# Stick-breaking softplus tiles split into a high and a low half for the triangle sums, with buffers laid out per phase

## The reference

```python
def block(i):                       # 128 queries
    z = jnp.einsum('bqhd,bshd->bhqs', qb, k).astype(jnp.float32) * dh ** -0.5
    ok = ((kpos[None, :] < qpos[:, None]) & valid[None, :])[None, None]
    log_1m = jnp.where(ok, -jax.nn.softplus(z), 0.0)
    after = lax.cumsum(log_1m, axis=3, reverse=True) - log_1m
    w = jnp.where(ok, jnp.exp(jax.nn.log_sigmoid(z) + after), 0.0)
    return jnp.einsum('bhqs,bshd->bqhd', w.astype(v.dtype), v)
od = stick_breaking(hd(dq, 8), hd(dk, 8), hd(dv, 8), valid)
od = od.reshape(bsz, P, -1) * jax.nn.silu(dg)
return jnp.concatenate([oc, od], axis=-1) @ w_out
```

## Time and profile before

| | |
|---|---|
| timed runs, median of 3 | 2760.39 us (2758.14 to 2762.59) |
| profiled execution | 2754.39 us, span 2752.6 us |
| TensorE matmul busy | 2623.4 us, 95% of the span |
| DVE / ACT / GpSimd busy | 38% / 32% / 39% |
| mean granted TensorE clock | 0.986 of full speed |
| the eight phases of stick-breaking | about 645 to 811 us |

### The profile page before, as it was taken

The page is one execution under the profiler, slowest core; times in us unless marked ns, Lnnn a source line. Parts: engine busy times, 40 slices in busy tenths (PEclk is TensorE's granted clock), DMA queues, the critical chain, the costliest instruction groups (busy, mean ns, idle before and its releaser), DMA issues.

```text
span 2752.6 us, 32062 instructions
## 1 busy us (share of the span) xinstructions
PE 2623.4 (95%) x13245; PEld 2134.7 (78%) x13245; DVE 1033.9 (38%) x1742; ACT 881.1 (32%) x1289; POOL 1068.3 (39%) x830
## 2 busy tenths in 40 slices
PE   7999898999996999999789999999999999999999
PEld 6888787886655888877667888878888888888887
DVE  4655355224335312145554222243121444421212
ACT  4432333225543222232534222232222322322221
POOL 3232232331114444443204444444444444454443
PEclk9999999999998999999999999999999999999999
DMA  4122001220012233221102332233322232223322
GB/s 129 59 62 82 28 24 54 77 77 32 23 39 91 89 94 105 92 87 59 58 9 92 100 97 94 88 96 98 101 92 92 92 104 95 92 92 95 104 92 77
DMA packets 215851, 217.78 MB, mean 79 GB/s; under 512 B 10599, under 2 KB 213090, under 8 KB 215706
## 3 DMA queue, kind: packets, MB, share of 16 engines
q1 hardware_dynamic: 215504, 215.68, 24.5%
q10 hardware_dynamic: 202, 0.06, 0.0%
HBM read 213.60 MB, written 2.12 MB: 78 GB/s over the span
## 4 chain that ended last, share of the span: by engine, by line
PE 86%; DVE 5%; ACT 4%; issue 2%; POOL 2%; DMA 1%; ACTq 0%; DVEq 0%; SPq 0%
PE ps L490 65%; PE ps L486 7%; PE ps L493 3%; POOL wl L466 2%; PE ps L804 2%; PE ps L773 1%; ACT wh L459 1%; PE ps L2021 1%; PE ps L1999 1%; PE ps L788 1%; DVE score L1587 1%; PE ps L2415 1%; DVE top L1586 0%; PE ps L1483 0%; PE ps L1980 0%
## 5 line engine op out<-in xcount | busy, mean ns | idle before, releaser
L466 POOL TENSOR_TENSOR wl<-raw,wh 128x512 fp32r<-128x512 f32 x794 | 1039.6, 1340 | 1591.3 <-ACT wh L459 1591.3
L490 PE MATMUL ps<-NH,wh 128*128 128x512 f32 (+1 forms) x1824 | 720.8, 395 | 38.1 <-POOL wl L466 27.8
L490 PE MATMUL ps<-NL,wh 128*128 128x512 f32 (+1 forms) x1824 | 715.4, 392 | 0.0
L490 PE MATMUL ps<-NH,wl 128*128 128x512 f32 (+1 forms) x1824 | 714.8, 392 | 0.0
L459 ACT ACTIVATE wh<-raw 128x2048 fp32r<-128x2048 f32 (+4 forms) x219 | 380.3, 1737 | 459.9 <-PE ps L490 413.6
L490 PEld LDWEIGHTS ps<-NH,wh 128*128 128x128 f32 (+1 forms) x1824 | 344.9, 189 | 119.9 <-POOL wl L466 30.9
L490 PEld LDWEIGHTS ps<-NH,wl 128*128 128x128 f32 (+1 forms) x1824 | 344.7, 189 | 74.3
L490 PEld LDWEIGHTS ps<-NL,wh 128*128 128x128 f32 (+1 forms) x1824 | 344.9, 189 | 73.6 <-issue 1.4
L490 PE MATMUL ps<-GH,wh 128*128 128x512 f32 x832 | 330.0, 397 | 3.0 <-DVE GL L728 2.3
L490 PE MATMUL ps<-GH,wl 128*128 128x512 f32 x832 | 332.6, 400 | 0.0
L490 PE MATMUL ps<-GL,wh 128*128 128x512 f32 x832 | 329.1, 396 | 0.0
(11 more groups left out here) (389 smaller groups left out, 3074.7 us busy)
## 6 DMA issues: line engine op xcount, KB each, us to landing
raw<-in_ffn_w_gate SPq DMA_DIRECT2D x44, 1024.0 KB, 5.3
raw<-in_ffn_w_up SPq DMA_DIRECT2D x44, 1024.0 KB, 5.3
raw<-in_ffn_w_down SPq DMA_DIRECT2D x32, 1024.0 KB, 4.9
raw<-in_w_in_ab SPq DMA_DIRECT2D x16, 1024.0 KB, 5.6
raw<-in_w_in_cd SPq DMA_DIRECT2D x14, 1024.0 KB, 5.0
raw<-in_ffn_w_down SPq DMA_DIRECT2D x16, 768.0 KB, 4.2
raw<-in_c_w_in SPq DMA_DIRECT2D x12, 1024.0 KB, 5.0
raw<-in_w_out_ab SPq DMA_DIRECT2D x8, 512.0 KB, 3.5
```

Of the source, the lines that this page charges most:

```text
L466: ins = nc.gpsimd.tensor_tensor(wl[:, b % 2, ks, 0:w], raw[:, b % 2, ks, 0:w], wh[:, b % 2, ks, 0:w].bitcast(F32), ALU.subtract)
L490: last = nc.tensor.matmul(ps[0:m1 - m0, bank, 0:SEQ], w[:, s, k, m0:m1], x(k), start=start, stop=stop)
```

## The change

The four softplus tiles of a phase are split. ACT copies each into `soft_hi` in F32R, DVE subtracts it from the tile in place into `soft_lo`, which lies over `soft`. The triangle product of line 1999 and the 128-column product of line 2001 are each done twice, on the high and on the low half, with copies of the constants in F32R. TensorE waits for `sb_soft_low`, no longer for `sb_soft`. The products on `later` stay as they are. Odd and even phases now use the same columns of `soft`, and `later` is laid out in 1152 columns instead of 1408.

```diff
-    soft = at("soft", 33984, [P, 2, 1920])
-    later = at("later", 37824, [P, 2, 1408])
+    soft = at("soft", 33984, [P, 2, 1152])
+    soft_lo = at("soft_lo", 33984, [P, 2, 1152], F32R)
+    soft_hi = at("soft_hi", 36288, [P, 2, 1024], F32R)
+    suffix_r = at("suffix_r", 51584, [P, P], F32R)
+    minus_r = at("minus_r", 51712, [P, P], F32R)
+    later = at("later", 38336, [P, 2, 1152])
...
-    SOFT_AT = ((128, 512), (512, 896), (896, 1408), (1408, 1920))
+    SOFT_AT = ((128, 512), (512, 896), (128, 640), (640, 1152))
...
-                pe.wait_ge(S("sb_soft"), n + 1)
-                nc.tensor.matmul(o[:, 0:w], const("suffix", 0, kn, kn), soft[0:kn, h, a:b], start=False, stop=False, skip_group_check=True)
+                pe.wait_ge(S("sb_soft_low"), n + 1)
+                nc.tensor.matmul(o[:, 0:w], suffix_r[0:kn, 0:kn], soft_hi[0:kn, h, a - P:b - P], start=False, stop=False, skip_group_check=True)
+                nc.tensor.matmul(o[:, 0:w], suffix_r[0:kn, 0:kn], soft_lo[0:kn, h, a:b], start=False, stop=False, skip_group_check=True)
                 if part == 0:
-                    last = nc.tensor.matmul(o[:, 256:384], const("minus_one"), soft[:, h, 128:256], start=False, stop=True, skip_group_check=True)
+                    nc.tensor.matmul(o[:, 256:384], minus_r[:, :], soft_hi[:, h, 0:P], start=False, stop=False, skip_group_check=True)
+                    last = nc.tensor.matmul(o[:, 256:384], minus_r[:, :], soft_lo[:, h, P:2 * P], start=False, stop=True, skip_group_check=True)
...
+        def low(n):
+            p, h, part = sb_task(n)
+            a, b = SOFT_AT[part]
+            kn = sb_rows(part)
+            dve.wait_ge(S("sb_soft_high"), n + 1)
+            if part < 3:
+                dve.wait_ge(S("sb_later"), 6 * p + 2 * part + h + 1)
+            nc.vector.tensor_tensor(soft_lo[0:kn, h, a:b], soft[0:kn, h, a:b], soft_hi[0:kn, h, a - P:b - P].bitcast(F32), ALU.subtract).then_inc(S("sb_soft_low"), 1)
...
-                    ins = nc.vector.memset(later[:, h, 384:512], 0.0)
+                    ins = nc.vector.memset(later[:, h, 512:640], 0.0)
+                nc.vector.tensor_copy(suffix_r[:, :], const("suffix"))
+                ins = nc.vector.tensor_copy(minus_r[:, :], const("minus_one"))
                 step(dve, ins)
             for g in range(2):
                 softplus(4 * f + 2 * g)
...
                     carry(f, 2 * (f % 2) + g, 1)
+            for j in range(4):
+                low(4 * f + j)
             for b, i in sb_between(f):
...
             if f == 0:
                 lin_high(act, ret, NT)
+            for j in range(4):
+                n = 4 * f + j
...
+                act.wait_ge(S("sb_soft"), n + 1)
+                nc.scalar.activation(soft_hi[0:kn, h, a - P:b - P], soft[0:kn, h, a:b], ACT.Copy).then_inc(S("sb_soft_high"), 1)
             for b, i in sb_between(f):
                 cd_act(act, b, i)
```

More of the change, by code:

```diff
@@ L1997, in sums @@
                 o = ps[0:kn, j, :]
-                pe.wait_ge(S("sb_soft"), n + 1)
-                nc.tensor.matmul(o[:, 0:w], const("suffix", 0, kn, kn), soft[0:kn, h, a:b], start=False, stop=False, skip_group_check=True)
+                pe.wait_ge(S("sb_soft_low"), n + 1)
+                nc.tensor.matmul(o[:, 0:w], suffix_r[0:kn, 0:kn], soft_hi[0:kn, h, a - P:b - P], start=False, stop=False, skip_group_check=True)
+                nc.tensor.matmul(o[:, 0:w], suffix_r[0:kn, 0:kn], soft_lo[0:kn, h, a:b], start=False, stop=False, skip_group_check=True)
                 if part == 0:
-                    last = nc.tensor.matmul(o[:, 256:384], const("minus_one"), soft[:, h, 128:256], start=False, stop=True, skip_group_check=True)
+                    nc.tensor.matmul(o[:, 256:384], minus_r[:, :], soft_hi[:, h, 0:P], start=False, stop=False, skip_group_check=True)
+                    last = nc.tensor.matmul(o[:, 256:384], minus_r[:, :], soft_lo[:, h, P:2 * P], start=False, stop=True, skip_group_check=True)
                 elif part == 1:
                     pe.wait_ge(S("sb_later"), 6 * p + h + 1)
-                    last = nc.tensor.matmul(o[:, 128:384], const("minus_one"), later[:, h, 128:384], start=False, stop=True, skip_group_check=True)
+                    last = nc.tensor.matmul(o[:, 128:384], const("minus_one"), later[:, h, 640:896], start=False, stop=True, skip_group_check=True)
                 elif part == 2:
                     pe.wait_ge(S("sb_later"), 6 * p + 2 + h + 1)
-                    last = nc.tensor.matmul(o[:, 128:512], const("minus_one"), later[:, h, 512:896], start=False, stop=True, skip_group_check=True)
+                    last = nc.tensor.matmul(o[:, 128:512], const("minus_one"), later[:, h, 128:512], start=False, stop=True, skip_group_check=True)
                 else:
                     pe.wait_ge(S("sb_later"), 6 * p + 4 + h + 1)
-                    last = nc.tensor.matmul(o, const("minus_one", 0, kn), later[:, h, 896:1408], start=False, stop=True, skip_group_check=True)
+                    last = nc.tensor.matmul(o, const("minus_one", 0, kn), later[:, h, 640:1152], start=False, stop=True, skip_group_check=True)
                 last.then_inc(S("sb_sum"), 1)
@@ L2062, in carry @@
             if part == 0:
-                ins = nc.vector.tensor_tensor(later[:, h, 128:384], soft[:, h, 256:512], soft[:, h, 0:256], ALU.add)
+                ins = nc.vector.tensor_tensor(later[:, h, 640:896], soft[:, h, 256:512], soft[:, h, 0:256], ALU.add)
             elif part == 1:
                 dve.wait_ge(S("sb_later"), 6 * (f // 2) + h + 1)
-                ins = nc.vector.tensor_tensor(later[:, h, 512:896], soft[:, h, 512:896], later[:, h, 0:384], ALU.add)
+                ins = nc.vector.tensor_tensor(later[:, h, 128:512], soft[:, h, 512:896], later[:, h, 512:896], ALU.add)
             else:
                 dve.wait_ge(S("sb_later"), 6 * (f // 2) + 2 + h + 1)
-                ins = nc.vector.tensor_tensor(later[:, h, 896:1408], soft[:, h, 896:1408], later[:, h, 384:896], ALU.add)
+                ins = nc.vector.tensor_tensor(later[:, h, 640:1152], soft[:, h, 128:640], later[:, h, 0:512], ALU.add)
             ins.then_inc(S("sb_later"), 1)
+        def low(n):
[6 more added lines that the diff above has]
+            nc.vector.tensor_tensor(soft_lo[0:kn, h, a:b], soft[0:kn, h, a:b], soft_hi[0:kn, h, a - P:b - P].bitcast(F32), ALU.subtract).then_inc(S("sb_soft_low"), 1)
         def gate(p):
```

## The result

The changed kernel takes 2775.7 us (median of 12) against 2761.9 for the kernel before, a ratio of 1.0063 with an interval of 1.0036 to 1.0090. Beside the kernel before on another chip it came to 1.0064 (1.0036 to 1.0092). It is slower, where 7.4 us were forecast: by 13.8 us between the medians, and by 17 us (10 to 25) by the ratio, which here is that of the means; two of the twelve executions of the changed kernel lie at 2791 and 2812 us and raise its mean.

A forecast was written before the change was run, and what follows sets the result against it. TensorE, with 86% of the last-ending chain, was taken as the bound. Stalls and ACT's delay less matmul gains made +4.4 us and clock drops +3; +7.4 on 2760.4 gave 2768 us, range 2757 to 2777.

The forecast's parts named there:

- wait for the low half, odd / phase 0: Ahead of the sums, TensorE waits for DVE's low half: 2.9 us in phases 3, 5, 7, 3.7 in phase 0.
- sums at full clock, odd / even: TensorE's sums shrink from 6.95 to 5.1 us in odd phases and from 3.70 to 2.5 in even ones.
- two rounded products of 128 columns: In the sums, two rounded 128-column products take 0.12 us, scaled from 512 columns; upper bound 0.44.
- phase 1: ACT's delayed silu and exponentials hold up z of phase 2, costing +2.4 us whatever the sums save.
- phases 2, 4, 6 together: Filler and value products hide the wait for the low half; shorter sums give -1.2 us each, -3.6 together.
- phases 3, 5, 7 together: 2.9 us of new stall less 1.85 of matmul gain costs +1.05 us each, +3.15 together.
- sum without the clock: Over the eight phases, +2.5 + 2.4 + 3.15 - 3.6 gives +4.4 us.
- the clock: Waits may halve TensorE's clock in phases 0, 3, 5, 7; estimate 3 us, bounds 0 and 6.4; hidden in phase 1.
- (a): Low halves come in time and TensorE keeps its gain: -8 us, 2752; milder form -3; chance together 0.10.
- (b): Stalls before the sums without clock drops: +4.4 us or a little less, 2763 to 2765; chance 0.24.
- (c): Four clock drops, GpSimd contention and 128-column products at 0.44 us all hit: +16 us, 2776; chance 0.11.
- (d): Rounded products in the sums do not run at the fast rate: 39 us above the forecast, 2807; chance 0.02.

The follow-up runs named there:

- fourth kernel: Changed kernel plus useless matmuls while TensorE waits for the low halves (16 in phase 0, 12 in phases 1, 3, 5, 7); 2770.7 us, 1.0034 of before.
- second kernel: Changed kernel still making and awaiting both halves, but with the plain 32-bit sums of the kernel before; 2787.4 us, 1.0108 of before.
- ninth experiment: Kernel before with the split in phases 2, 4, 6 alone, plus five useless matmuls in a phase 0 wait; ratio 0.9999 to before, phase 0 24.8 us.
- fifth kernel: Changed kernel with DVE's lows of the first two tasks moved ahead of the last two tasks' softplus; 2772.9 us, 1.0048 of before.
- third: Changed kernel without low halves or rounding copies: softplus written directly rounded, second product of each pair against zeros; 2757.2 us, 0.9987 of before.
- seventh: Softplus and running sum written once rounded, no low halves or products against zeros, every sum product one rounded matmul; 2751.3 us, 0.9977 of before.

## Why the prediction was wrong, by its steps

| step | worked out | measured |
|---|---|---|
| first sum behind the first softplus, odd phases | 4.4 us | 4.34 (phase 1) |
| wait for the low half, odd / phase 0 | 2.9 / 3.7 us | 2.6 to 2.8 / 4.1 |
| sums at full clock, odd / even | 5.1 / 2.5 us | 5.4 / 2.51 (fourth kernel) |
| two rounded products of 128 columns | 0.12 us | 0.17 |
| phase 0 without the clock | +2.5 us | +2.7 |
| phase 1 | +2.4 us | +2.4 |
| phases 2, 4, 6 together | -3.6 us | -3.5 |
| phases 3, 5, 7 together | +3.15 us | +4.1 |
| sum without the clock | +4.4 us | +5.7 |
| the clock | +3 us (0 to 6.4) | +12.0 |
| the phases | +7.4 us | +17.7 |

**The mechanism of the waits was right.** The wait for the low half, its places, the cover in the even phases, and ACT as the limit behind phase 1 are as forecast; the fourth kernel, in which the clock stays up in all phases but 0, reproduces every phase within 0.6 us. Its +5.7 us against my +4.4 comes mainly from the odd sums, which took 5.4 us and not 5.1: where the two kinds of product alternate each takes a little more than single rows had shown, as the 384-column one on `later` ahead of a rounded one, 0.74 us instead of 0.64 (726.95 to 727.69 in phase 3). GpSimd's subtraction met the lows in phase 7 alone, as said: there the four took 3.58 us instead of 2.48, and nobody waited for it. The two 128-column products came out at 0.17 us; my scaled row was 0.05 too low, and the even sums still took 2.51. The Trainium skill ("TensorE: Matmul & The Clock Gate", Back-to-back issue gap) states about 81 ns for each such matmul in a stream with weight loads, an estimate of 0.16 us for two, and the trace agrees.

**The step that failed was the clock,** "Estimate 1.8 x 1.6 = 3 us, bounds 0 and 6.4": it measured 12.0 us in the phases, by the fourth kernel. Three things were wrong in it.

First the number of falls. I gave waits of 2.9 us four chances in ten, since 3.57 us at 1336.87 had left the clock up. It fell behind all five, in both profiles. Why there is open. Dense 512-column filler follows both waits of rows 6 (behind the second from 1337.70 on, behind eight small products), and the clock fell behind one of them; the second kernel's four odd waits, with the same sums behind them, brought two falls. So the work behind a wait doesn't explain it, and one row in which the clock stays up was too little to set a chance by.

Then the price of a fall. I priced it with filler, in one stretch of 3.4 us. That held in phases 3 and 5 (granted clock 0.76 over the sums), which cost 1.6 each. In phases 1 and 7 the sums stayed slow as long as they lasted: the granted clock was 0.56 from 719.3 to 728.5 and 0.57 from 842.1 to 851.1. The last sums took 9.0 us instead of 5.5, and phase 7 cost 3.5 us more than with spares. Phase 0 cost 2.6, and phase 2 another 1.0, since it began at half clock.

Last the cover in phase 1: "in phase 1 ACT's delay hides it". With the clock up z waited 1.8 us for the exponentials, but the slow sums overran that by 1.8 us (19.9 against 18.1).

**The bounds were too tight for the same reasons**: 6.4 was four falls at 1.6 us. There were five, at 1.6 to 3.5 us, and one of them ran on into phase 2.

**The median came nearer than the mechanism.** 2775.7 was measured and 2768 forecast, a miss of 7.7 us, while the phases missed by 10.3. That the timed difference is the smaller one is no merit of the sum.

**The rivals.** (a), the kernel that keeps its gain, did not appear, nor did (b), the case without falls. Of (c), the slow one at +16 us, the total was nearest, but for another cause: no 128-column product at 0.44 and no contention on an awaited low. (d) is out: two 384-column rounded products took 0.35 us together (782.21 to 782.56 in phase 4), as scaled.

## What to carry to other kernels

When an edit adds a wait on TensorE's path, price what stands behind the wait at both clocks, not filler, and don't count on a fall staying away because one was absent behind a wait as long elsewhere: here five waits of 14.8 us in all, mostly paid for by shorter matmuls, cost 12 us more through the clock in the profiled phases. Filling a wait with useless matmuls shows that price in one run. It was itself a gain here (7.3 us between the medians, 12.0 in the phases), but can be one only where the work behind the wait is not held by another engine: in the ninth experiment filler that ended sooner met another wait. And split operands only in the stages in which the operand's producer has slack of more than the added steps; here three of eight.

## What the runs showed that I had not expected

A wait of 2.58 us for one operand was followed by half clock (phase 3 of the changed kernel), while one of 2.79 us ahead of like work was not (phase 7 of the second kernel), nor were 1.4 to 1.6 us in the odd phases (fifth kernel). TensorE at work does not by itself have its clock back: over the sums of phase 1 it was busy for 9.16 of 9.20 us at a granted clock of 0.56. A shorter stage can be slower: with less matmul work in phase 1 the third, fifth and seventh kernels waited 2.4 to 4.75 us for the exponentials and paid for it with 3.3 to 4.7 us in phase 2. And unchanged instructions from about 390 to 450 us ran wholly at half clock in some executions of either kernel, 27 us for the kernel before.
